# Keys of both windowed attentions made feature tile by feature tile in 4 or 6 banks, with tables and clearing on GpSimd

## The chip, the cores and the metric

One core of one Trainium2 chip runs the kernel as a single launch. The metric is the device time in microseconds (us); lower is better. The kernel before was timed in three runs.

## What is computed

Two networks of two layers each, on 512 tokens of width 1024 (all float32), one behind the other:

```python
def reference(...):
    x = first_block(x, ...)      # diff attention, swiglu, shared kv + windowed attention with sinks, swiglu
    return second_block(x, ...)  # conv mixers, conv ffn, windowed attention with context, conv ffn
```

The change lies in the two windowed attentions. The first one (`shared_kv` and `swa_sink_attention` of the first network; tag "a" in the kernel) makes keys and values of the normed 512 tokens, 4 key heads of width 64. Keys and queries are normed per head and rotated by the positions:

```python
k, v = jnp.split(rms_norm(x, kv_norm) @ w_kv, 2, axis=-1)
k = apply_rope(rms_norm(k.reshape(B, S, SW_KV_HEADS, HEAD_DIM), k_norm), cos, sin)
q = apply_rope(rms_norm((h @ w_q).reshape(...), q_norm), cos, sin)
```

The second one (`windowed_gqa`; tag "b") makes keys and values of 512 tokens and of 256 context tokens (6 token tiles of 128), without the per-head norm, and rotates only the 4 tiles of tokens:

```python
q, k, v = jnp.split(h @ w_qkv, [Q_W, Q_W + KV_W], axis=-1)
kc, vc = jnp.split(hc @ w_qkv[:, Q_W:], [KV_W], axis=-1)
```

In both, each of 16 query heads sees a window of key tiles, and a sink logit joins the softmax.

## The kernel before, in words

Five engine programs are written out by hand and meet at semaphores: SP issues the loads, PE (TensorE) multiplies, ACT (ScalarE) and DVE (VectorE) evacuate and compute, POOL (GpSimd) takes the powers for the norms. All of them walk through the list `stages` that `make_plan` (L53) writes: for the first attention a late norm, `kv` (2 weight blocks: keys, values), `q` (4 blocks), `resid`; for the second a full norm, then the same.

Every float32 product is three matmuls: the rounded (high) parts of both operands, and each high part with the other's low part. So each weight block is split before use: ACT writes `w_hi` (`split`, L658), DVE writes the rest, `w_lo` (`split`, L1193; with a gain per feature tile through `low_weights`, L1206, eight operations). `s_lo` counts the blocks whose low parts are ready, `s_mm` those whose slot can be overwritten. SP loads a block of queries once the low parts of the block before in its slot are written (L468).

`kv` on PE (L2106): 2*nt projections (nt = 4 or 6 token tiles), keys of all tiles first, then values, by `project256` (L2092): for one token tile, eight feature tiles of three matmuls with 256 columns. They alternate between banks 0 and 1, so projection n waits for the evacuation of n-2 (`kpe`). The first one waits for each feature tile of the hidden states (`s_h`). Behind projections 2 to nt PE turns the keys of a tile (`turn`, L2110: four transposes of what DVE has rotated, into banks 4 and 5), and the last turn stands at the end of the stage. The first attention's sums of squares for the norm of x (`sum_squares`, L1868) run behind projection 0; its root scales rows at the evacuation.

`kv` on ACT (L920): `split(st, 1, 1)`, then per projection a copy and a square (keys, L946 and L949) or two copies into `sw_va` and `sw_vb` (values, L953 and L955), which must have been cleared (`vzero`); the turned keys' high part (L926); the query blocks' `split` 0 ahead of the values and 1 at the end, ahead of the last turned keys.

`kv` on DVE (L1625), in this order: clearing of `sw_va` and `sw_vb` (L1629, L1630); in the first attention the rotation tables of queries and keys (`rope_tables`, L1179: 32 products of 32 columns); the negated sinks (L1640); the low parts of the value weights; then per token tile the mean squares (first attention only, L1489), the rotation (L1500, L1502, L1668), the doubled keys (L1671 or L1673) and the low part of the keys turned before (`k_low`, L1644). The low parts of query blocks 0 and 1 are made behind tile nt-2 and behind the last tile, the latter ahead of the last `k_low`.

`q` (`swa`: PE L2135, ACT L965, DVE L1693): PE waits at L2245 and L2246 for all evacuated values and all key low parts, projects query tiles 0 and 1 into bank 0, turns them, and then works in 32 half steps of scores, turned exponentials, values and the projection of a later query tile. DVE per query tile: mean squares, rotation (`rotated`, L1697), `doubled`, `q_low` (L1716), and per half step the `maxima` (L1722). Query tile 4 is the first to need query block 1.

In the full norm (DVE L1449, ACT L810), DVE forms the means, waits for the roots that GpSimd takes (L523) and PE spreads, and then makes the hidden states feature tile by feature tile (L1479, L1470).

Of the kernel before, what the change touches and what calls it, by code (L numbers as in the profile page):

```python
# [11 lines left out]
ALU = mybir.AluOpType  # L12
# [3 lines left out]
P = 128  # L16
# [5 lines left out]
HD = 64  # L22
# [30 lines left out]
def make_plan():  # L53
# [93 lines left out]
    norm(gain="final_norm", toks=SEQ, final=True)  # L147
    ring = [st for st in stages if "nb" in st]
# [18 lines left out]
def program(nc, dram, out):  # L167
    stages = make_plan()
    stack = ExitStack()
    with stack:  # L170
# [22 lines left out]
        small = sbuf("small", [P, 64])  # L193
# [17 lines left out]
        neg_sink = sbuf("neg_sink", [P, 16])  # L211
# [306 lines left out]
        def _(pool):  # L518
# [56 lines left out]

            angles()
# [3 lines left out]
            for st in stages:  # L580
# [4 lines left out]
                elif st["kind"] == "heads":  # L585
# [34 lines left out]
        def _(act):  # L620
# [189 lines left out]
            def norm(st):  # L810
                for kt in range(KT_D):
# [107 lines left out]

            def kv(st):  # L920
                S = s_swt[st["tag"]]
                nt = 6 if st["ctx"] else 4

                def turned(t):
                    act.wait_ge(S["ktr"], t + 1)
                    act.activation(sw_k[:, :, t * P:(t + 1) * P],  # L926
                                   pb[:, 4 + t % 2, :].rearrange("p (g n) -> p g n", g=4), ACT.Copy).then_inc(S["khi"], 1)
                    act.drain()
# [5 lines left out]
                split(st, 1, 1)  # L934
                if st.get("late"):
                    act.wait_ge(s_pw, st["late"]["rms0"] + 1)
                for n in range(2 * nt):
                    t = n % nt
                    if n == nt:
                        split(st["after"], 0, 0)  # L940
                        act.wait_ge(S["vzero"], 1)
                    act.wait_ge(S["kpj"], n + 1)
                    if n < nt:
                        if n >= 2:
                            act.wait_ge(S["krope"], n - 1)
                        act.activation(kv_buf(st, 512 + 256 * (n % 2), 768 + 256 * (n % 2)), pb[:, n % 2, 0:256], ACT.Copy,  # L946
                                       scale=root(t))
                        act.drain()
                        r = act.activation(kv_buf(st, 1024 + 256 * (n % 2), 1280 + 256 * (n % 2)), pb[:, n % 2, 0:256],  # L949
                                           ACT.Square, scale=root(t))  # L950
                    else:
                        at = HD * (2 * t + 1)
                        act.activation(sw_va[:, :, at:at + HD], pb[:, n % 2, 0:P].rearrange("p (g f) -> p g f", g=2), ACT.Copy,  # L953
                                       scale=root(t))
                        r = act.activation(sw_vb[:, :, at:at + HD],  # L955
                                           pb[:, n % 2, P:2 * P].rearrange("p (g f) -> p g f", g=2), ACT.Copy,
# [3 lines left out]
                    if 3 <= n <= nt + 1:  # L960
                        turned(n - 3)
# [1422 lines left out]
```

## Time and profile before

| | us |
|---|---|
| median of 3 runs | 3028.74 (3027.15 to 3029.84) |
| the profiled execution's own time | 3028.09 |
| its span in the profile | 3026.3 |
| PE busy | 2786.0 (92%) |
| DVE busy | 1836.8 (61%) |
| ACT busy | 1080.0 (36%) |
| POOL busy | 118.8 (4%) |

The mean granted clock of PE over the span is 0.955 of full speed. A busy PE in the profile is a PE with matmuls in flight. Idle time of an engine costs only where another one waits for it. The stretches of this case are the first attention's keys, values and first queries, from about 724 to 802 us of the span, and the second's, from about 2280 to 2371 us. "PEclk" is the granted clock as a share of full speed, "issue" is a wait for which the profile names no engine, and a row of the timeline gives start, duration, engine, line, operation, its tiles, and in brackets the idle time before it with the operation that ended it.

### The profile page before, as it was taken

The numbers are of one execution on the slowest core, as the hardware profiler recorded it, in microseconds if no ns is written. First come the engines' busy times: TensorE is split into PE (matmuls) and PEld (weight loads), VectorE is DVE, ScalarE is ACT, GpSimd is POOL, SyncE is SP. The second block draws the span as 40 slices with busy tenths as digits, with TensorE's granted clock in tenths as the row PEclk, the third lists the DMA queues.
The fourth block names the chain that finished last, engine by engine and source line by source line (L and its number), as shares of the span: only waits on it lengthen the run. The fifth ranks groups of instructions, "written<-read, shape, count | busy, mean of one in ns | idle before, by whom it ended". The sixth has DMA issues, their size and how long they took to land.

```text
span 3026.3 us, 41051 instructions
## 1 busy us (share of the span) xinstructions
PE 2786.0 (92%) x14220; PEld 2339.0 (77%) x14220; DVE 1836.8 (61%) x2910; ACT 1080.0 (36%) x1778; POOL 118.8 (4%) x148
## 2 busy tenths in 40 slices
PE   7999899997787999998986899999997899899998
PEld 6777788886676788887875788888886787688886
DVE  6766567676565577667996554353455455564645
ACT  5444332223565322223112232232223566352432
POOL 4111000000110000000000000000000000000000
PEclk8999999998898999998997999999998999999999
DMA  3111254452001355542110122122111000232321
GB/s 110 63 56 43 98 187 167 171 182 72 29 29 36 112 180 174 175 155 68 56 49 30 48 70 70 56 65 68 54 58 42 15 29 8 70 97 91 97 89 65
DMA packets 69314, 252.07 MB, mean 83 GB/s; under 512 B 7840, under 2 KB 10144, under 8 KB 66592
## 3 DMA queue, kind: packets, MB, share of 16 engines
q1 hardware_dynamic: 69152, 249.99, 24.5%
q8 instruction: 92, 1.51, 0.2%
q14 instruction: 70, 0.57, 0.1%
HBM read 247.87 MB, written 2.10 MB: 83 GB/s over the span
## 4 chain that ended last, share of the span: by engine, by line
PE 61%; DVE 16%; issue 15%; ACT 4%; DVEq 2%; POOLq 0%; ACTq 0%; POOL 0%; DMA 0%; SPq 0%
PE psum L1852 16%; PE psum L1851 16%; PE psum L1853 16%; DVE work L1372 4%; PE psum L2233 2%; DVE w_lo L1201 1%; ACT work L991 1%; PE psum L1991 1%; ACT sw_pt L1003 1%; PE psum L1969 1%; PE psum L1971 1%; PE psum L1970 1%; DVE neg_max L1740 1%; DVE tok_ms L1489 1%; DVE w_lo L1566 1%
## 5 line engine op out<-in xcount | busy, mean ns | idle before, releaser
L1851 PE MATMUL psum<-hx_hi,w_hi 128*128 128x512 f32 x1568 | 623.9, 398 | 28.9 <-DVE w_lo L1201 13.5
L1852 PE MATMUL psum<-hx_lo,w_hi 128*128 128x512 f32 x1568 | 625.1, 399 | 0.0
L1853 PE MATMUL psum<-hx_hi,w_lo 128*128 128x512 f32 x1568 | 623.7, 398 | 0.0
L675 ACT ACTIVATE w_hi<-w_raw 128x1024 fp32r<-128x1024 f32 (+1 forms) x328 | 344.6, 1051 | 527.2 <-PE psum L1853 231.4
L1201 DVE TENSOR_TENSOR w_lo<-w_raw,w_hi 128x1024 fp32r<-128x1024 f32 (+1 forms) x328 | 397.7, 1212 | 192.6 <-ACT w_hi L675 174.0
L1851 PEld LDWEIGHTS psum<-hx_hi,w_hi 128*128 128x128 f32 x1568 | 297.1, 189 | 79.1 <-issue 16.7
L1853 PEld LDWEIGHTS psum<-hx_hi,w_lo 128*128 128x128 f32 x1568 | 297.1, 189 | 69.9
L1852 PEld LDWEIGHTS psum<-hx_lo,w_hi 128*128 128x128 f32 x1568 | 298.0, 190 | 48.4
L1851 PE MATMUL psum<-a_hi,w_hi 128*128 128x512 f32 (+1 forms) x656 | 234.1, 357 | 18.1 <-DVE a_lo L1313 10.0
L1852 PE MATMUL psum<-a_lo,w_hi 128*128 128x512 f32 (+1 forms) x656 | 234.8, 358 | 0.0
L1853 PE MATMUL psum<-a_hi,w_lo 128*128 128x512 f32 (+1 forms) x656 | 233.9, 357 | 0.0
L1851 PE MATMUL psum<-o_hi,w_hi 128*128 128x512 f32 x544 | 217.8, 400 | 5.6 <-DVE o_lo L1778 3.9
L1852 PE MATMUL psum<-o_lo,w_hi 128*128 128x512 f32 x544 | 216.8, 398 | 0.0
L1853 PE MATMUL psum<-o_hi,w_lo 128*128 128x512 f32 x544 | 216.7, 398 | 0.0
L1335 DVE SCALAR_TENSOR_TENSOR work<-psum,vec,work 128x511 f32<-128x511 f32 (+1 forms) x132 | 83.2, 658 | 164.3 <-ACT work L758 156.3
L523 POOL TENSOR_TENSOR tok_r<-tok_ms,half 128x4 f32<-128x4 f32 (+1 forms) x70 | 71.8, 1025 | 2502.2 <-DVE tok_ms L1115 1949.6
L1277 DVE SCALAR_TENSOR_TENSOR X<-psum,mods,X 128x512 f32<-128x512 f32 x96 | 60.6, 658 | 178.6 <-PE psum L1853 177.1
L1851 PEld LDWEIGHTS psum<-a_hi,w_hi 128*128 128x128 f32 x656 | 125.2, 191 | 38.5 <-DVE a_lo L1313 10.5
L758 ACT ACTIVATE work<-psum,vec 128x768 f32<-128x768 f32 (+1 forms) x88 | 70.0, 795 | 223.5 <-PE psum L1853 215.8
L1852 PE MATMUL psum<-hc_lo,w_hi 128*128 128x256 f32 x512 | 144.8, 283 | 0.0
L1851 PE MATMUL psum<-hc_hi,w_hi 128*128 128x256 f32 x512 | 144.8, 283 | 0.0
L1853 PE MATMUL psum<-hc_hi,w_lo 128*128 128x256 f32 x512 | 144.5, 282 | 0.0
(289 smaller groups left out, 4914.2 us busy)
## 6 DMA issues: line engine op xcount, KB each, us to landing
mod_w<-in_w_mod SPq DMA_DIRECT2D x96, 512.0 KB, 3.6
w_raw<-in_fup SPq DMA_DIRECT2D x88, 512.0 KB, 4.5
w_raw<-in_cup SPq DMA_DIRECT2D x88, 512.0 KB, 3.5
w_raw<-in_fdown SPq DMA_DIRECT2D x32, 512.0 KB, 4.6
w_raw<-in_cdown SPq DMA_DIRECT2D x32, 512.0 KB, 3.5
w_raw<-in_da_qkv SPq DMA_DIRECT2D x6, 1536.0 KB, 6.5
w_raw<-in_fdown SPq DMA_DIRECT2D x16, 384.0 KB, 3.1
w_raw<-in_cdown SPq DMA_DIRECT2D x16, 384.0 KB, 3.0
```

Source lines behind the costliest of these rows:

```text
L523: pool.tensor_tensor(tok_r[:, a:b], tok_ms[:, a:b], half[:, a:b], ALU.pow).then_inc(done, 1)
L675: r = act.activation(w_hi[:, off:off + n], w_raw[:, raw:raw + n], ACT.Copy)
L758: act.activation(wk[:, s, 0:toks], ps_of(st, s, 0, toks), ACT.Copy, scale=vec[:, bass.ds(b + col, 1)]).then_inc(s_ctap, 1)
L991: r = act.activation(work[:, e:e + (w1 - w0)], psum[:, w0:w1], ACT.Exp, bias=neg_max[:, col:col + 1], scale=root, accum_out=row_sum[:, col ...
L1201: r = dve.tensor_tensor(w_lo[:, off:off + n], w_raw[:, raw:raw + n], w_hi[:, off:off + n].bitcast(F32), ALU.subtract)
L1277: r = dve.scalar_tensor_tensor(X[:, b, a:e], ps_of(st, s, a, e), mods[:, l, c, bass.ds(b + o, 1)], X[:, b, a:e], ALU.mult, ALU.add)
L1335: dve.scalar_tensor_tensor(dst[:, a + 1:e], src(a, e - 1), prev, dst[:, a + 1:e], ALU.mult, ALU.add)
L1372: dve.scalar_tensor_tensor(acc, u[:, j:j + n], w, acc, ALU.mult, ALU.add)
L1851: pe.matmul(dst, wh, xh, start=first, stop=False)
L1852: pe.matmul(dst, wh, xl, start=False, stop=False)
L1853: return pe.matmul(dst, wl, xh, start=False, stop=last)
L2233: r = pe.matmul(pb[:, 5, 0:256], v_cols(tiles[k], g, p % 2), sw_pt[:, n % 2, 256 * i:256 * i + 256], start=p % 2 == 0 and k == 0, stop=p % ...
```

## The change

Keys: PE walks over the eight feature tiles and multiplies each for all 4 or 6 token tiles, one bank per token tile, so that all key projections end together. Values: as before one token tile after the other, each into its own bank, with the turn of the key tile before behind it (now in banks 6 and 7). The last turn moves into the query stage, behind its first projection, and the wait for all values and key low parts moves behind its second. The sums of squares of the late norm run behind feature tile 3. The mark that frees the second weight slot moves from the last turn to the first query projection.

GpSimd takes over the clearing of `sw_va` and `sw_vb`, the rotation tables of the first attention's queries and keys (8 products of 128 columns instead of 32 of 32) and the negated sinks, each in an earlier stage. The low and high parts of the value weights in the second attention move ahead of the norm's wait for roots. Those of query block 0 come behind key tile 1 (ACT: ahead of tile 2), those of query block 1 into the query stage: on ACT between the first and the second turned query tile, on DVE behind the first two query tiles and ahead of the first maxima.

```diff
+    for st, after in zip(stages, stages[1:]):
+        if st["kind"] == "norm" and after["kind"] == "kv" and not st.get("late"):
+            st["kv"] = after
...
-        small = sbuf("small", [P, 64])
+        rope_g = sbuf("rope_g", [P, 2, 96])
...
-        neg_sink = sbuf("neg_sink", [P, 16])
+        neg_sink = sbuf("neg_sink", [P, 2, 16])
...
+            def rope_gains():
+                for which, (name, scale) in enumerate((("sw_q_norm", HD ** -0.5), ("k_norm", 1.0))):
+                    pool.tensor_scalar(rope_g[:, which, 0:HD], rows(name), scale, None, ALU.mult)
+                pool.drain()
+                for which in range(2):
+                    pool.tensor_scalar(rope_g[:, which, HD:96], rope_g[:, which, 32:HD], -1.0, None, ALU.mult)
+                for which, name in enumerate(("sinks1", "sinks2")):
+                    pool.tensor_scalar(neg_sink[:, which, :], rows(name), -1.0, None, ALU.mult)
+                pool.drain()
+
+            def rope_tables():
+                for which, tab in ((0, swa_tab[:]), (1, k_tab)):
...
+                    for c, h, gain in ((0, 0, g0), (0, 1, g1), (1, 0, g1_neg), (1, 1, g0)):
+                        r = pool.tensor_tensor(tab[:, c, :, h, :], gain, trig[:, c], ALU.mult)
+                r.then_inc(s_tabs, 1)
+                pool.drain()
...
+                    rope_gains()
+                    pool.memset(sw_vb[:], 0.0)
+                elif st.get("w") == "fup0_2":
+                    pool.wait_ge(s_modd, MOD_TILES)
+                    rope_tables()
+                    pool.wait_ge(s_mm, st["block0"])
+                    pool.memset(sw_va, 0.0).then_inc(s_swt["a"]["vzero"], 1)
...
+                elif st["kind"] == "kv":
+                    pool.wait_ge(s_mm, st["block0"])
+                    pool.memset(sw_va, 0.0)
+                    pool.memset(sw_vb[:], 0.0).then_inc(s_swt["b"]["vzero"], 1)
```

In the diff of ACT, `norm` begins with the split of the value weights (second attention), and `kv` and `swa` change as follows:

```diff
             def norm(st):
+                if st.get("kv"):
+                    split(st["kv"], 1, 1)
...
-                split(st, 1, 1)
                 if st.get("late"):
+                    split(st, 1, 1)
                     act.wait_ge(s_pw, st["late"]["rms0"] + 1)
                 for n in range(2 * nt):
                     t = n % nt
+                    if n == 2:
+                        split(st["after"], 0, 0)
                     if n == nt:
-                        split(st["after"], 0, 0)
                         act.wait_ge(S["vzero"], 1)
...
                     if 3 <= n <= nt + 1:
-                        turned(n - 3)
-                split(st["after"], 1, 1)
-                turned(nt - 1)
+                        keys_turned(st, n - 3)
...
                 evac_proj(0)
+                keys_turned(st["before"], (6 if st["ctx"] else 4) - 1)
+                evac_proj(1)
                 turned(0)
-                evac_proj(1)
+                split(st, 1, 1)
                 turned(1)
```

On DVE:

```diff
                 if st.get("late"):
                     return
+                if st.get("kv"):
+                    split(st["kv"], 1, 1)
                 dve.wait_ge(s_rb, st["norm0"] + 1)
...
-                dve.memset(sw_va, 0.0)
-                dve.memset(sw_vb[:], 0.0).then_inc(S["vzero"], 1)
-                if not st["ctx"]:
...
-                            rope_tables(tc, ts, gain, 1, t)
-                dve.tensor_scalar(neg_sink[:], rows("sinks2" if st["ctx"] else "sinks1"), -1.0, None, ALU.mult)
-                dve.drain()
-                split(st, 1, 1)
+                if st.get("late"):
+                    split(st, 1, 1)
+                    dve.wait_ge(s_tabs, 5)
...
-                    if t:
-                        k_low(t - 1)
-                    if t == nt - 2:
+                    if t == 1:
                         split(st["after"], 0, 0)
-                split(st["after"], 1, 1)
+                    if t >= 2:
+                        k_low(t - 2)
+                k_low(nt - 2)
                 k_low(nt - 1)
...
                     rotated(m)
                     doubled(m)
                     q_low(m)
+                split(st, 1, 1)
                 for p in range(35):
```

On PE:

```diff
-                for n in range(2 * nt):
-                    if n % nt == 0:
-                        pe.wait_ge(s_lo, st["block0"] + n // nt + 1)
-                    if n >= 2:
-                        pe.wait_ge(S["kpe"], n - 1)
...
-                    if n == 0 and st.get("late"):
+                pe.wait_ge(s_lo, st["block0"] + 1)
+                for k in range(KT_D):
+                    pe.wait_ge(s_h, 8 * (hset[0] - 1) + k + 1)
+                    w = slice(256 * k, 256 * (k + 1))
+                    for t in range(nt):
+                        if k == 0:
+                            pe.wait_ge(s_ev, st["lin0"] + 1 + (t // 2 if st["ctx"] else t))
+                        xh, xl = h_tile(k, t)
+                        dst = pb[:, t, 0:256]
+                        pe.matmul(dst, xh, w_hi[:, w], start=k == 0, stop=False)
+                        pe.matmul(dst, xl, w_hi[:, w], start=False, stop=False)
+                        r = pe.matmul(dst, xh, w_lo[:, w], start=False, stop=k == KT_D - 1)
+                        if k == KT_D - 1:
+                            r.then_inc(S["kpj"], 1)
+                    if k == 3 and st.get("late"):
                         sum_squares(st["late"])
-                    if 2 <= n <= nt:
-                        turn(n - 2)
-                turn(nt - 1)
+                pe.wait_ge(s_lo, st["block0"] + 2)
+                for t in range(nt):
+                    pe.wait_ge(S["kpe"], t + 1)
+                    project256(pb[:, t, 0:256], t, 1, s_mm if t == 0 else None).then_inc(S["kpj"], 1)
+                    if t:
+                        turn_keys(st, t - 1)
...
+                pe.wait_ge(S["kpe"], nt + 1)
+                project(0)
+                turn_keys(st["before"], nt - 1)
+                project(1)
                 pe.wait_ge(S["kpe"], 2 * nt)
                 pe.wait_ge(S["klo"], nt)
-                project(0)
-                project(1)
                 turn_q(0)
```

## Rows read from the trace of the kernel before

**Rows 1.** Windows: PE, PEld, DVE, ACT, POOL busy us (count), PEclk, DMA share, GB/s
```profile
core 0: us, PE busy (x) PEld busy (x) DVE busy (x) ACT busy (x) POOL busy (x), PEclk, DMA share, GB/s
11.40:22.40 11.00, 11.00 (x64) 10.75 (x62) 8.05 (x12) 7.46 (x14) 8.99 (x16) 1.00 0.93 358
754.30:758.90 4.60, 4.57 (x22) 4.57 (x23) 2.59 (x6) 0.95 (x2) 1.01 (x1) 0.50 0.23 98
758.90:763.20 4.30, 4.23 (x36) 4.03 (x35) 1.31 (x4) 3.01 (x7) 0.04 (x1) 1.00 0.01 4
830.30:834.40 4.10, 4.09 (x17) 3.73 (x18) 3.36 (x9) 1.91 (x5) 1.55 (x2) 0.58 0.00 0
684.00:700.00 16.00, 16.00 (x70) 12.85 (x70) 5.44 (x7) 3.94 (x6) 0.00 (x0) 1.00 0.24 75
2480.00:2500.00 20.00, 19.32 (x141) 17.23 (x140) 10.56 (x27) 12.65 (x28) 0.65 (x1) 1.00 0.01 1
724.10:799.30 75.20, 46.42 (x298) 44.67 (x298) 45.45 (x115) 23.18 (x53) 7.05 (x7) 0.75 0.17 56
2294.90:2368.40 73.50, 56.18 (x392) 53.05 (x393) 39.57 (x59) 24.70 (x48) 0.00 (x0) 0.81 0.13 44
```

**Rows 2.** Waits of PE, 724 to 800: who for whom, total us, times, longest
```profile
PE psum L2116 <- DVE kv_tmp L1671: 14.4, 2, 12.1
PE psum L2152 <- issue: 7.8, 1, 7.8
```

**Rows 3.** Waits of PE, 2280 to 2370
```profile
PE psum L2099 <- DVE hc_lo L1470: 12.7, 8, 3.8
PE psum L2152 <- issue: 5.3, 1, 5.3
```

**Rows 4.** Timeline, DVE, first attention: start us, us, operation, idle before
```profile
729.08 0.69 DVE L1274 TENSOR_TENSOR X<-psum,X 128x512 f32<-128x512 f32 x1
...
735.50 1.45 DVE L1629 MEMSET sw_va<- 128x1664 f32 x1 [0.47 <-issue]
...
747.94 3.25 DVE L1209 SCALAR_TENSOR_TENSOR w_lo<-w_raw,vec,w_hi 128x256 fp32r<-128x256 f32 x8 [0.42 <-issue]
...
751.29 0.42 DVE L1489 TENSOR_REDUCE tok_ms<-kv_tmp 128x4 f32<-128x256 f32 x1
...
754.37 0.42 DVE L1489 TENSOR_REDUCE tok_ms<-kv_tmp 128x4 f32<-128x256 f32 x1
...
801.89 0.42 DVE L1489 TENSOR_REDUCE tok_ms<-sw_sq 128x4 f32<-128x256 f32 x1
```

**Rows 5.** Timeline, ACT and DVE, first attention
```profile
736.70 0.47 ACT L949 ACTIVATE kv_tmp<-psum,tok_r 128x256 f32<-128x256 f32 x1
...
800.12 0.69 DVE L1718 TENSOR_TENSOR sw_qb<-psum,sw_qa 128x512 fp32r<-128x512 f32 x1 [1.73 <-ACT sw_qa L981]
```

**Rows 6.** Timeline, DVE and PE, second attention
```profile
2291.15 2.37 DVE L1479 SCALAR_TENSOR_TENSOR work<-X,gains,psum 128x512 f32<-128x512 f32 x4 [4.42 <-PE psum L1860]
...
2309.63 0.58 PE L2099 MATMUL psum<-w_hi,hx_hi 128*128 128x256 f32 x1 [1.46 <-DVE hc_lo L1470]
...
2310.33 0.48 DVE L1470 SCALAR_TENSOR_TENSOR hc_lo<-work,mods,hc_hi 128x256 fp32r<-128x256 f32 x1
...
2314.57 2.29 DVE L1201 TENSOR_TENSOR w_lo<-w_raw,w_hi 128x2048 fp32r<-128x2048 f32 x1
2316.95 0.42 DVE L1500 TENSOR_TENSOR work<-work,axial 128x256 f32<-128x256 f32 x1
...
2318.74 0.42 DVE L1500 TENSOR_TENSOR work<-work,axial 128x256 f32<-128x256 f32 x1
...
2370.11 0.69 DVE L1731 TENSOR_REDUCE neg_max<-psum 128x1 f32<-128x512 f32 x1
```

**Rows 7.** Lines by themselves: count, duration ns min/median/max, starts; last modulation sum
```profile
L1145 DVE TENSOR_TENSOR w_lo<-w_raw,w_hi x8: 558/810/822, 7.6 to 26.2; 128x384 fp32r<-128x384 f32 x8
...
L571 POOL TENSOR_TENSOR da_tab_c<-work,trig x4: 642/832/1432, 24.1 to 37.2; 128x128 f32<-128x128 f32 x4
...
682.75 1.22 DVE L1224 SCALAR_TENSOR_TENSOR mod_out<-mod_w,mod_c 128x1024 f32<-128x1024 f32 x1
```

More of the change, by code:

```diff
@@ L574, in head_table @@
                 pool.drain()
+            k_tab = kv_tmp[:, 2560:3072]
+            def rope_gains():
[9 more added lines that the diff above has]
+                for which, tab in ((0, swa_tab[:]), (1, k_tab)):
+                    tab = tab.rearrange("p (c t h f) -> p c t h f", c=2, t=4, h=2)
+                    g0, g1, g1_neg = (rope_g[:, which, a:a + 32].unsqueeze(1).broadcast_to([P, 4, 32]) for a in (0, 32, HD))
+                    for c, h, gain in ((0, 0, g0), (0, 1, g1), (1, 0, g1_neg), (1, 1, g0)):
+                        r = pool.tensor_tensor(tab[:, c, :, h, :], gain, trig[:, c], ALU.mult)
+                r.then_inc(s_tabs, 1)
+                pool.drain()
             angles()
@@ L918, in heads, with keys_turned @@
                 outputs_high(7)
+            def keys_turned(st, t):
+                S = s_swt[st["tag"]]
+                act.wait_ge(S["ktr"], t + 1)
+                act.activation(sw_k[:, :, t * P:(t + 1) * P],
+                               pb[:, 6 + t % 2, :].rearrange("p (g n) -> p g n", g=4), ACT.Copy).then_inc(S["khi"], 1)
+                act.drain()
             def kv(st):
@@ L1176, in modulation @@
                                                      vec[:, o:o + 8], ALU.add, ALU.mult)
-                dve.drain()
-            def rope_tables(tab_c, tab_s, gain, n, t):
-                g = gain.rearrange("p (n h f) -> p n h f", n=n, h=2)
-                cos, sin = over(trig[:, 0, t, :], n), over(trig[:, 1, t, :], n)
-                tc = tab_c.rearrange("p n (h f) -> p n h f", h=2)
-                ts = tab_s.rearrange("p n (h f) -> p n h f", h=2)
-                for h in range(2):
-                    dve.tensor_tensor(tc[:, :, h, :], g[:, :, h, :], cos, ALU.mult)
-                    dve.drain()
-                dve.scalar_tensor_tensor(ts[:, :, 0, :], g[:, :, 1, :], -1.0, sin, ALU.mult, ALU.mult)
-                dve.drain()
-                dve.tensor_tensor(ts[:, :, 1, :], g[:, :, 0, :], sin, ALU.mult)
                 dve.drain()
@@ L1695, in swa @@
                 t1, t2 = sw_t[:, 0, :], sw_t[:, 1, :]
+                sinks = neg_sink[:, 1 if st["ctx"] else 0, :]
                 def rotated(m):
@@ L2104, in project256, with turn_keys @@
                 return r
+            def turn_keys(st, t):
+                S = s_swt[st["tag"]]
+                pe.wait_ge(S["krope"], t + 1)
+                if t >= 2:
+                    pe.wait_ge(S["klo"], t - 1)
+                for g in range(4):
+                    o = 1536 + 512 * (t % 2) + P * g
+                    r = pe.transpose(pb[:, 6 + t % 2, g * P:(g + 1) * P], kv_buf(st, o, o + P), ident[:])
+                r.then_inc(S["ktr"], 1)
             def kv(st):
@@ L2108, in kv @@
                 nt = 6 if st["ctx"] else 4
-                def turn(t):
-                    pe.wait_ge(S["krope"], t + 1)
-                    if t >= 2:
-                        pe.wait_ge(S["klo"], t - 1)
-                    for g in range(4):
-                        o = 1536 + 512 * (t % 2) + P * g
-                        r = pe.transpose(pb[:, 4 + t % 2, g * P:(g + 1) * P], kv_buf(st, o, o + P), ident[:])
-                        if t == nt - 1 and g == 0:
-                            r.then_inc(s_mm, 1)
-                    r.then_inc(S["ktr"], 1)
@@ L2151, in project @@
                         dst = pb[:, 0, 0:256]
-                        pe.matmul(dst, xh, w_hi[:, off:off + 256], start=k == 0, stop=False)
+                        r = pe.matmul(dst, xh, w_hi[:, off:off + 256], start=k == 0, stop=False)
+                        if m == 0 and k == 0:
+                            r.then_inc(s_mm, 1)
                         pe.matmul(dst, xh, w_lo[:, off:off + 256], start=False, stop=False)
```

37 lines of the change are left out of this document (9 added, 28 removed).

## The prediction, made before the changed kernel ran

> **What bounds the kernel now.** The page comes first: span 3026.3 us, PE busy 92%, and a chain that is 61% PE, 16% DVE and 15% "issue". So most stretches are full and only holes in PE can be won. The two stretches that the change touches are holes: between the last block of the stage before and the first scores of the query stage PE is busy for 46.4 of 75.2 us in the first attention, at a granted clock of 0.75, and for 56.2 of 73.5 us in the second, at 0.81 [rows 1]. The waits say on whom. In the first, PE stands 14.4 us in the two transposes of turned keys behind DVE's L1671, 12.1 of it at once, and 7.8 us ahead of the first query projection [rows 2]; no engine is named there, but project(0) stands behind waits on the last key low part, and DVE gives that only behind the low parts of the second query block. In the second, 12.7 us go to the hidden states, one feature tile after the other, and 5.3 ahead of the query projection [rows 3]. The timeline says what DVE did meanwhile: from 735.50 it cleared, made tables and split weights, and took the first key tile at 751.29, though ACT had it by 737.2 [rows 4, 5].
>
> **The clock.** After each hole PE runs at 1.2 GHz first: 22 matmuls in 4.6 us (0.21 each) at clock 0.50, then 36 in 4.3 us (0.119 each) at 1.00, which is 2.4 GHz [rows 1]. I use 4.6 us at 0.21, then 0.119; another low stretch is 4.1 us [rows 1].
>
> **First attention, step by step.** PE starts the keys as before, at 726.7. Feature tile 0 now goes through four banks, and the fourth waits until the residual in bank 3 is evacuated: DVE's L1274 at 729.08 ends at 729.8 [rows 4]. Nine matmuls fit ahead; 1.9 us of idle are added here. Of the other 87, 22 run low (to 734.4), 65 take 7.7 us and the sums of squares, now after feature tile 3, 1.0: the keys end at 743.1. The first token tile is done a microsecond earlier, 742.0, some 9 us later than today. That is paid, since nothing could use it sooner. Means and roots come by 739 and DVE splits the second block (3.3 us [rows 4]) by 742.3, both ahead of it.
> ACT copies and squares a tile in 1.0 us (0.47 each and a gap [rows 5]), so DVE starts at 743.0 and not at 751.3. Its queue then sets the pace: four tiles of 3.08 us (751.29 to 754.37 [rows 4]), the first query block's low parts 3.3, and four key low parts of 0.8 each (a 512-wide difference, 0.69 [rows 5], and a gap), together 18.8: 761.8. PE's own queue meanwhile (four value projections of 24 matmuls, 2.85 each, transposes, project(0)) needs some 18 us and waits 2 to 3 us in pieces of 1, which I take as too short to lower the clock. The hole ahead of the queries is gone, as project(0) asks only for the first evacuated value.
> Then rotation of query tile 0 on DVE 2.6 (a key tile less its 0.4 us addition), transposes and ACT's copy 1.4 (DVE waited 1.73 [rows 5], and part of that was PE's other work), low part 0.8, and the same again for tile 1: 771.4. Now the moved piece: query block 1's low parts, 3.3 us, stand ahead of the first maxima, with PE behind them (scores of half 1 need the first exponentials): 774.7. Maxima 1.0: DVE rotates query tile 2 at 775.7. Today it does at 801.89 [rows 4]. **Gain 26.2.**
>
> **Second attention.** Hidden states come every 2.47 us (1.0 of matmuls and a wait of 1.46 today) and the last low part ends at 2310.8 [rows 6]; those DVE steps stay. PE did 3 matmuls for each of them, now it does 18: 22 in the first 4.6 us from 2294.9, then 122 at 0.119 = 14.5: 2314.0, which is later than the last data plus 18 matmuls (2313.0), so PE's count sets it. The low parts of block 1 (2.29 [rows 6]) move to DVE's wait for the roots (4.42 us up to 2291.15 [rows 6]) and cost nothing; without that wait they would cost 2.3. Six values and five transposes: 6 x 2.85 + 5 x 0.36 = 18.9, then project(0), one transpose and project(1) with a 0.2 us wait, 6.3: 2339.2. DVE has 15.6 us of work here (four tiles of 1.79, 2316.95 to 2318.74 [rows 6], two copies, six low parts, one 2.3 split) and is ahead. Query tiles 0 and 1 by the same chain without means (rotation 1.8, hand-over 1.4, low part 0.8; the first rotation beside project(1)): 2339.2 + 2.2 + 4.0 = 2345.4. Low parts of block 1, 2.4: first maxima at 2347.8, today 2370.11 [rows 6]. **Gain 22.3.** The stage behind is full (PE 19.3 of 20 us at clock 1.00 [rows 1]), so the shift stays.
>
> **Given back.** Ahead of the exponentials PE will stand some 3 us in both stages. After such a hole in today's first query stage it ran at clock 0.58 for 4.1 us [rows 1], worth 1.7 us of a full PE: I take 1.5 in the second and 1.0 in the first, where PE has holes anyway.
>
> **GpSimd.** No row shows a clear of this size there. DVE takes 1.45 [rows 4]; GpSimd's dearest 128x128 product takes 1.43 [rows 7], by 13 (1664 columns) 18.6. A clear lies between, and eight table products take 5 to 11 (0.64 to 1.43 each). Covers: tables and one clear start once the modulation is summed, at 684 [rows 7], and are asked for at 742; the other clear and the gains follow the heads stage, with all of a feed-forward behind them; the second attention's pair starts at 2288.2 and is asked for at 2327 (even 2 x 18.6 arrives at 2325). If that cover went, ACT and PE would wait for the difference. What they do to DVE is the unknown: the first weights' low parts took 0.56 at best and 0.81 in the median while GpSimd worked [rows 7], 45% more. Lower end 0 (a release of DVE is already counted), upper end 20 us of the second norm at 45%, 9 us. I take 0.5, since what GpSimd does there is clearing, and DVE's longest operation there reads PSUM.
> The Trainium skill, SBUF — State Buffer (Who interferes with whom), says that a VectorE instruction with two SBUF inputs contends with a GpSimd one that reads SBUF, but not with one that only writes. By that rule the term would be 0.0; the 0.56 to 0.81 beside reading GpSimd operations agrees with it, and no row shows the writing side.
>
> **Sum.** 26.2 + 22.3 - 2.5 - 0.5 = 45.5, off the profiled execution's 3028.1: 2982.6. The median of the runs is 0.6 above that execution: **2983**.
>
> **Rivals.** (a) *Keys at the low clock* (0.08). The keys now change bank after every three matmuls, and PE is fed in portions in the second attention. If it stayed at 1.2 GHz, the first keys cost 65 x 0.094 = 6.1 more and the second 144 x 0.2125 = 30.6, 11.6 more: 3000. Against it: the first projections of the kernel run the same loop, four banks, three matmuls each, and have 64 matmuls of 384 columns in 11 us at clock 1.00 [rows 1]. The Trainium skill, TensorE: Matmul & The Clock Gate (A second HAM failure mode: psum-queue depth-cycling), describes a kernel whose clock moved to and fro because PE cycled through banks; by its rule the time would be this rival's, and this trace does not bear it out.
> (b) *The new hole ahead of the first maxima lasts on* (0.07). If both query stages ran at 0.58 for 20 us and not 4, 8 us more in the full one and 4 in the other: 2995. For it: the 3.3 and 2.4 us stand ahead of everything; against: clock 1.00 a few us behind the hole in [rows 1].
> (c) *GpSimd shuts DVE out: slower* (0.03). Place: the 37 us of clears in the second norm, where DVE sets the pace, and 30 us of tables and clear at 684. There DVE is busy 5.4 of 16 us under a full PE [rows 1], which hides about 10. With every operation at its dearest and DVE stopped throughout: 37 + 20 = 57 lost against 49 won : 3036. It decides only once over 46 us are lost, five times the 9 above.
> (d) *Nothing moves* (0.02): PE is held through the evacuations or the roots so that DVE starts at 751 as before: 3029. A wait for the second block (742.3) would have to slip 9 us.
> The forecast itself has 0.80; within it the length of the low stretches (1 us either way, twice), the 1.4 us hand-over (1.7 at most, four times) and the waits in pieces give 2975 to 2990. With (b) inside and (c), (d) and most of (a) outside, the range is 2975 to 2997. A measurement of this kernel tells about 0.2%, 6 us, from no change: faster 0.95 (forecast, a, b), same 0.02, slower 0.03.
>
> **What the profile after would show.** Right: no clears or 32-wide products on DVE; the first mean of a key tile near 743; the wait behind L1671 falls from 14.4 to about 2 and that ahead of project(0) is gone; keys of the second attention in one stretch from 2295 minus the first gain to 19 us later; about 1.9 us of idle within the first feature tile; about 3 us ahead of the second scores. Wrong: clock 0.50 throughout the keys (a); 0.58 beyond 5 us in the query stages (b); clears near 18 us or DVE's norm steps longer than 2.47 a pair (c); DVE's first tile behind 746, or PE waiting for hidden states in portions as now.

## Result and profile after

| | before | changed |
|---|---|---|
| median of the runs beside each other | 3029.09 us (3027.15 to 3029.84, 4 runs) | 2992.51 us (2988.13 to 2997.06, 4 runs) |
| span of the profiled execution | 3026.3 | 2995.2 |

The ratio is 0.988 (95% interval 0.9865 to 0.9895): 36.6 us faster where 46 were forecast, inside the range. A later series of the same kernel gave 2989.73 (4 runs); the median of all eight is 2991.0.

The windows of the changed kernel, with the columns of [rows 1]: the stretch from the first key to the rotation of query tile 2 in the first attention, its slow beginning and the full stretch behind it, the stretch behind the hole ahead of the exponentials, and the second attention from its first key to its first maxima.
```profile
734.24:783.84 49.60, 41.38 (x318) 39.86 (x318) 35.11 (x77) 26.00 (x58) 7.06 (x7) 0.94 0.19 66
734.24:740.50 6.26, 5.41 (x23) 5.12 (x24) 5.53 (x8) 4.15 (x9) 0.00 (x0) 0.50 0.49 168
740.50:749.00 8.50, 8.50 (x75) 8.50 (x74) 3.42 (x9) 1.46 (x4) 1.01 (x1) 1.00 0.00 0
784.99:788.10 3.11, 2.40 (x10) 2.00 (x11) 2.09 (x7) 1.05 (x4) 0.59 (x1) 0.50 0.60 253
2285.39:2339.09 53.70, 52.07 (x414) 50.98 (x414) 35.12 (x57) 25.12 (x50) 0.00 (x0) 0.96 0.06 21
```
Both stretches took 75.21 us before (726.68 to 801.89, 2294.90 to 2370.11); they take 49.59 and 53.70 now. PE is busy for 83% of the first and 97% of the second, at a clock of 0.94 and 0.96 instead of 0.75 and 0.81 [rows 1].

Who PE waits for, 731.6 to 808 us, answering to [rows 2]:
```profile
PE psum L2192 <- DVE sw_dup L1730: 3.4, 5, 1.2
PE psum L2246 <- ACT work L1028: 3.1, 1, 3.1
PE psum L2145 <- DVE w_lo L1234: 2.5, 1, 2.5
PE psum L2129 <- DVE sw_k L1663: 1.7, 2, 0.9
```
The 14.4 and 7.8 us are gone. What is left are pieces near 1 us, the wait ahead of the first key, which was there before, and one new hole of 3.1 us ahead of the exponentials. DVE, GpSimd and PE in the timeline, answering to [rows 4, 5]:
```profile
694.02 2.43 POOL L596 TENSOR_TENSOR kv_tmp<-rope_g,trig 128x128 f32<-128x128 f32 x4
696.59 1.49 POOL L630 MEMSET sw_va<- 128x1664 f32 x1
...
734.24 0.58 PE L2145 MATMUL psum<-w_hi,hx_hi 128*128 128x256 f32 x1 [2.55 <-DVE w_lo L1234]
...
750.35 0.42 DVE L1516 TENSOR_REDUCE tok_ms<-kv_tmp 128x4 f32<-128x256 f32 x1 [2.35 <-ACT kv_tmp L988]
...
779.49 3.25 DVE L1234 SCALAR_TENSOR_TENSOR w_lo<-w_raw,vec,w_hi 128x256 fp32r<-128x256 f32 x8
782.84 0.42 DVE L1757 TENSOR_REDUCE neg_max<-psum 128x2 f32<-128x256 f32 x1
783.83 0.42 DVE L1516 TENSOR_REDUCE tok_ms<-sw_sq 128x4 f32<-128x256 f32 x1
```
DVE now waits for ACT at its first key tile instead of making tables, and the moved low parts stand directly ahead of the first maxima.

The two stages gained 25.6 and 21.5 us, 47.1 together. The span fell by 31.1 only. The table cuts each profiled span at four instructions: PE's first key of the first attention (K1), DVE's rotation of query tile 2 (Q), PE's first key of the second (K2), DVE's first maxima there (M). It holds the experiments too; the times are starts and differences of starts in us, all from the traces. The medians come from three series on three chips, and the kernel before was timed in each: 3028.3 us beside after_again, before_again, addr_shift and split_late, 3028.3 beside after_placed, aligned, pool_only and keys_only, 3030.0 beside shift64, shift512, best and undo_placed. Each ratio below is to the kernel before in its own series.

| kernel | start to K1 | K1 to Q | Q to K2 | K2 to M | M to end | median |
|---|---|---|---|---|---|---|
| before | 726.68 | 75.21 | 1493.01 | 75.21 | 656.2 | 3029.1 |
| before_again | 727.40 | 75.33 | 1493.20 | 75.12 | 656.2 | 3029.2 |
| changed | 734.24 | 49.59 | 1501.56 | 53.70 | 656.1 | 2992.5 |
| after_again | 727.20 | 50.55 | 1499.84 | 53.45 | 658.4 | 2989.7 |
| addr_shift | 731.09 | 75.94 | 1495.98 | 74.10 | 657.3 | 3035.9 |
| shift64 | 726.45 | 75.25 | 1499.00 | 75.68 | 653.9 | 3032.4 |
| shift512 | 729.80 | 75.76 | 1493.37 | 75.28 | 654.1 | 3028.1 |
| after_placed | 728.03 | 50.51 | 1493.78 | 53.47 | 656.4 | 2983.6 |
| aligned | 727.18 | 50.53 | 1496.45 | 53.54 | 653.5 | 2985.5 |
| pool_only | 731.35 | 59.81 | 1492.87 | 75.14 | 653.5 | 3012.4 |
| keys_only | 725.09 | 61.57 | 1496.55 | 53.47 | 658.5 | 2998.6 |
| split_late | 730.18 | 46.18 | 1501.43 | 51.16 | 655.2 | 2986.7 |
| best | 727.33 | 47.16 | 1496.88 | 51.08 | 656.7 | 2979.1 |
| undo_placed | 725.50 | 51.18 | 1493.73 | 54.31 | 653.6 | 2982.5 |

So the changed kernel's first profile lost 7.6 us ahead of K1 and 8.6 between Q and K2, in stages that the change does not touch. That was the first question.

### The profile page after: what moved, and what is told of

Same layout as the page of the kernel before. It is cut to its first block, busy times and chain, and to the rows that moved or that the text cites. A ratio compares the mean times of both kernels' runs of the same rounds, so it can differ in the third digit from the quotient of the medians.

```text
span 2995.2 us, 40999 instructions
## 1 busy us (share of the span) xinstructions
PE 2789.4 (93%) x14220; PEld 2338.0 (78%) x14220; DVE 1825.8 (61%) x2871; ACT 1081.1 (36%) x1778; POOL 131.6 (4%) x166
## 3 DMA queue, kind: packets, MB, share of 16 engines
q1 hardware_dynamic: 69152, 249.99, 24.7%
## 4 chain that ended last, share of the span: by engine, by line
PE 62%; DVE 16%; issue 15%; ACT 4%; DVEq 2%; POOLq 1%; POOL 0%; ACTq 0%; DMA 0%; SPq 0%
PE psum L1869 16%; PE psum L1870 16%; PE psum L1871 16%; DVE work L1397 4%; PE psum L2257 2%; DVE w_lo L1226 1%; ACT work L1028 1%; PE psum L2009 1%; ACT sw_pt L1040 1%; PE psum L1987 1%; PE psum L2246 1%; PE psum L1988 1%; PE psum L1989 1%; DVE w_lo L1593 1%; DVE tok_ms L1516 1%
```

## Experiments: where 16 us went

**The same kernels again.** No edit.

> The changed kernel once more. In its first profile the two attention stages gained 25.6 and 21.5 us, 47.1 together, but the span fell by 31.1 only: 7.6 us were gone before the keys of the first attention (between the heads stage and 734 us) and 8.6 us between the two attentions, where a block of the last feed-forward took 8.48 us instead of 8.40 at clock 1.00. Theory of chance: those 16 us belong to that one execution; a second profile shows the keys near 727 to 730 and a span near 2985. Theory of the code (placement of the buffers or of the work): both losses come again within 1 us, keys at 734 and a block of 8.48 us, and the median stays at 2990 to 2995.

Measured 2989.73 us (2986.64 to 2992.55). The theories split: the loss ahead of the keys was of that execution, the one between the attentions came again (6.8 of 8.6 us). PE's first key in the second profile of the changed kernel:
```profile
727.20 0.39 PE L2145 MATMUL psum<-w_hi,hx_hi 128*128 128x256 f32 x1 [2.55 <-DVE w_lo L1234]
```

> The kernel before once more, for the spread of its own stages. Theory of chance: its keys of the first attention start anywhere from 727 to 734 us and its block of the last feed-forward takes 8.40 to 8.48. Theory of the code: 726.7 within 1 us and 8.40 again; the time 3029 within 3 us in either case.

Measured 3029.18 us (3026.3 to 3032.82, 10 runs), ratio to its own series 1.0003 (0.9993 to 1.0012). K1 727.40 and Q to K2 1493.20: the part between the attentions repeats within 0.2 us. K1 lies between 725.1 and 734.2 in the fourteen profiles, with no order by kernel, so the first profile's 7.6 us are put down to its execution. K1 goes with the granted clock ahead of it: summed up to K1, PE stood at clock 0.50 for 54.6 us in the profiles with K1 at 725.1 and 725.5, for 58.0 in the first profile of the kernel before (726.7), and for 79.1 in the first of the changed kernel (734.2); the others lie between, in nearly this order. Why the clock differs from one execution to the next stays open.

**The kernel before with its buffers moved.** The change makes one table larger (`small`, 64 columns, becomes `rope_g`, 192) and doubles `neg_sink`; both are allocated ahead of the working tiles and the hidden states, which so move by 512 and 576 bytes. Their addresses were read from the compiled programs; the sizes of the tiles, each rounded up to 32 bytes, add up to the same place within 128 bytes.
```
-        small = sbuf("small", [P, 64])
+        small = sbuf("small", [P, 192])
-        neg_sink = sbuf("neg_sink", [P, 16])
+        neg_sink = sbuf("neg_sink", [P, 32])
```

> The kernel before with two small tables made larger, so that all later buffers lie 512 or 576 bytes further on, as they do in the changed kernel; nothing else differs. Theory that placement costs the 16 us outside the attentions: a block of the last feed-forward takes 8.48 us instead of 8.40, the keys of the first attention start near 734 us instead of 727, and the time is 3040 to 3045. Rival, that placement does nothing: 3029 within 3 us.

Measured 3035.86 us (3031.41 to 3038.86, 11 runs), ratio 1.0021 (1.0012 to 1.003): slower by 7.6 us, with the same instructions on the same shapes. That is less than the 11 to 16 expected and more than the rival's 3. The trace has only 3.0 of it between Q and K2, and 4.4 ahead of K1, which scatters by as much anyway.

**Which of the two moves.** Each line of that edit by itself.

> The kernel before with its hidden states and operands 64 bytes further on (they begin 96 bytes behind a multiple of 128, as in the changed kernel), the working tiles where they were. Theory that the place of the moving operands within 128 bytes makes the difference: a block of the last feed-forward takes 8.48 us instead of 8.40, time 3034 to 3036, like the shift of 512 and 576 bytes. Rival, that it is the 512 bytes (the working tiles, the distance to the weights): 8.40 us and 3028.

> The kernel before with working tiles and hidden states 512 bytes further on (the hidden states begin 32 bytes behind a multiple of 128, as before). Theory that the place within 128 bytes decides: 8.40 us a block and 3028. Rival, that the distance does: 8.48 us and 3034 to 3036.

Measured: 64 bytes 3032.44 us (ratio 1.0012, 1.0002 to 1.0021), 512 bytes 3028.14 us (0.9997, 0.9988 to 1.0007). The 64 bytes cost 2.5 us and not the 4 to 6 more that were expected, and 2.5 and -1.8 do not add up to the 7.6 of both together. The medians alone leave this open; the traces are sharper. DVE's weight split in a block of the feed-forward ahead of the second attention (the "last feed-forward" of the expectations), and the fiftieth split after it (one a block nearly throughout), in the kernel before, with 64 bytes, and in the changed kernel:
```profile
1738.90 1.23 DVE L1201 TENSOR_TENSOR w_lo<-w_raw,w_hi 128x1024 fp32r<-128x1024 f32 x1 [0.26 <-ACT w_hi L675]
...
2156.42 1.23 DVE L1201 TENSOR_TENSOR w_lo<-w_raw,w_hi 128x1024 fp32r<-128x1024 f32 x1 [0.18 <-ACT w_hi L675]
```
```profile
1739.50 1.23 DVE L1201 TENSOR_TENSOR w_lo<-w_raw,w_hi 128x1024 fp32r<-128x1024 f32 x1 [0.26 <-ACT w_hi L675]
...
2160.62 1.23 DVE L1201 TENSOR_TENSOR w_lo<-w_raw,w_hi 128x1024 fp32r<-128x1024 f32 x1 [0.18 <-ACT w_hi L675]
```
```profile
1723.84 1.23 DVE L1226 TENSOR_TENSOR w_lo<-w_raw,w_hi 128x1024 fp32r<-128x1024 f32 x1 [0.26 <-ACT w_hi L710]
...
2145.33 1.23 DVE L1226 TENSOR_TENSOR w_lo<-w_raw,w_hi 128x1024 fp32r<-128x1024 f32 x1 [0.18 <-ACT w_hi L710]
```
417.5, 421.1 and 421.5 us; the 8.40 and 8.48 of the expectations were read off single blocks. With 512 bytes (1742.94 to 2160.50) it is 417.6. So in this stretch the place within 128 bytes decides: the hidden states begin 32 bytes behind a multiple of 128 in the kernel before, 96 in the changed one. All fourteen profiles sort by it: 417.3 to 417.6 us in the eight at 32 bytes, 421.1 to 421.5 in the five at 96, 419.7 in the one at 0 (further down). The starts of the matmuls show where. In 407 steps of six matmuls each (512, 512, 512, 256, 256, 256 columns), with PE at clock 1.00 and no waits, a step takes 1.050 us on average in every profile at 32 bytes and 1.060 in every one at 96; the first of the six has most of it (0.230 against 0.237). Over the stretch's some 400 steps that is the 4 us.

From that last split to K2 the profiles sort the same way: 138.3 to 138.7 us at 32 bytes, 140.0 to 140.1 at 96. The first part of Q to K2, up to the first of the splits, takes 934.5 to 941.0 us with no order by place. So the column Q to K2 mixes two things: the place, worth 5.2 us between after_again and after_placed (3.6 and 1.6), and a scatter of several us that is not explained. keys_only and best have the old place and still show 1496.6 and 1496.9.

**The changed kernel with every buffer where it was.** The two tables go behind the last buffer.
```
-        rope_g = sbuf("rope_g", [P, 2, 96])
+        small = sbuf("small", [P, 64])
-        neg_sink = sbuf("neg_sink", [P, 2, 16])
+        neg_sink1 = sbuf("neg_sink", [P, 16])
...
+        _, rope_g, neg_sink2 = layout(("tail_gap", [P, 24 * D], F32), ("rope_g", [P, 2, 96], F32), ("neg_sink2", [P, 16], F32))
```

> The changed kernel with its two new tables put behind the last buffer, so that every other buffer lies at the address that it has in the kernel before; the instructions are the same. The kernel before with its buffers shifted took 7.6 us more, and its feed-forward of both token sets took 8.48 us a block where the kernel before took 8.40, as in the changed kernel. Theory that this placement took back 6 us of the gain: a block takes 8.40 us again, the time is 2984 to 2985 against the 2991 of the changed kernel (median of its 8 runs so far). Rival, that the loss comes with the changed program itself (code, queues): 8.48 us and 2990.

Measured 2983.6 us (2983.01 to 2984.12), ratio 0.9852 (0.9837 to 0.9867). 50 splits take 417.5 again and Q to K2 1493.8: the theory of placement holds.
```profile
1716.38 1.22 DVE L1228 TENSOR_TENSOR w_lo<-w_raw,w_hi 128x1024 fp32r<-128x1024 f32 x1 [0.26 <-ACT w_hi L712]
...
2133.87 1.23 DVE L1228 TENSOR_TENSOR w_lo<-w_raw,w_hi 128x1024 fp32r<-128x1024 f32 x1 [0.19 <-ACT w_hi L712]
```

**Would a full boundary be better still?**
```
         sw_sum = sbuf("sw_sum", [P, 4])
+        pad = sbuf("pad", [P, 8])
```

> The changed kernel with one unused tile of 32 bytes more ahead of the hidden states, which so begin at a multiple of 128 bytes; before they begin 32 bytes behind one, in the changed kernel 96. Theory that a matmul's reading costs more where its data begin off such a boundary: the six matmuls of a step of the feed-forward of both token sets, 1.057 us before and 1.065 changed, take 1.05 or less, the pure 512-column stages gain too, and the time is below 2985. Rival, that only the order of addresses against the weights matters and 32 bytes do nothing: 1.065 us and 2991.

Measured 2985.46 us (2983.01 to 2993.21), no gain over the 2983.6 at 32 bytes. 50 splits take 419.7 us and a step of six matmuls 1.055, both between the other two places, so there theory and rival missed. But where all matmuls have 512 columns the theory was right in most stages. The same splits in the feed-forward behind the second attention, first in after_placed (70.62 us), then here (70.34):
```profile
2745.04 1.23 DVE L1228 TENSOR_TENSOR w_lo<-w_raw,w_hi 128x1024 fp32r<-128x1024 f32 x1 [0.16 <-issue]
...
2815.66 1.23 DVE L1228 TENSOR_TENSOR w_lo<-w_raw,w_hi 128x1024 fp32r<-128x1024 f32 x1 [0.51 <-ACT w_hi L712]
```
```profile
2744.99 1.22 DVE L1227 TENSOR_TENSOR w_lo<-w_raw,w_hi 128x1024 fp32r<-128x1024 f32 x1 [0.17 <-issue]
...
2815.33 1.23 DVE L1227 TENSOR_TENSOR w_lo<-w_raw,w_hi 128x1024 fp32r<-128x1024 f32 x1 [0.51 <-ACT w_hi L711]
```
Six matmuls of 512 columns without a wait take 1.400 us at clock 1.00 in all thirteen profiles at 32 or 96 bytes. At 0 they take 1.394 from 950 to 1390 us and from 2650 to 2990, but 1.400 from 350 to 730, where the hidden states lie at the same place. So the fastest place for the mixed stage is not the one for the even stages, and the place alone does not set the pace. By an estimate from these numbers the even stages win some 3 us at 0 and the mixed one loses as much. Why is open: 32 and 96 stand the same to a multiple of 64 and still differ in the mixed stage, so a line of 64 bytes read once more is not it.

## Experiments: what each part of the change is worth

**GpSimd's part alone** (buffers in place): the kernel before without the clears and tables at the head of DVE's key stage, and with the changed kernel's GpSimd code.
```
-                dve.memset(sw_va, 0.0)
-                dve.memset(sw_vb[:], 0.0).then_inc(S["vzero"], 1)
...
+                dve.wait_ge(s_tabs, 5)
```

> The kernel before with the tables, clears and sinks on GpSimd as in the change, its two new tables behind the last buffer; the keys are made token tile by token tile and the low parts stay where they were. Theory: DVE reaches the first key tile of the first attention some 12 us sooner (739.3 instead of 751.3), the wait of PE behind L1671 falls from 14.4 to 2 or 3 us and no other wait takes its place, gain 11 to 12; nothing in the second attention; 3017. Rival, that PE's own sequence holds it next: 5 us or less, 3023.

Measured 3012.43 us (3011.57 to 3017.64), ratio 0.9951 (0.9937 to 0.9965): a gain of 15.9. K1 to Q falls by 15.4, K2 to M by nothing. The waits of PE, 720 to 806 us:
```profile
PE psum L2175 <- issue: 7.8, 1, 7.8
...
PE psum L2139 <- DVE kv_tmp L1693: 2.3, 1, 2.3
```
14.4 fell to 2.3 as expected: 12.1. The other 3 us go with the clock. Over the stage (K1 to Q) it is 0.83 and not 0.75, and PE is busy for 44.6 us with the same 307 matmuls that took 47.8 before (47.0 in before_again). The theory had left that term out. The stage before and in this kernel:
```profile
726.68:801.89 75.21, 47.83 (x307) 45.96 (x308) 44.36 (x112) 25.38 (x57) 7.05 (x7) 0.75 0.17 56
731.35:791.15 59.80, 44.57 (x307) 42.95 (x308) 35.08 (x76) 25.39 (x57) 7.05 (x7) 0.83 0.21 71
```

**The order alone** (tables, clears and sinks back on DVE, at the head of its key stage; buffers in place).
```
+                dve.memset(sw_va, 0.0)
+                dve.memset(sw_vb[:], 0.0).then_inc(S["vzero"], 1)
...
-                dve.wait_ge(s_tabs, 5)
```

> The changed kernel with tables, clears and sinks back on DVE at the head of the key stage, and every buffer where it is before: so only the order of keys, turns and low parts is changed. Theory: in the first attention DVE takes the first key tile 24 us after PE's first key, as before (16 in the changed kernel), what follows it is as short as in the changed kernel (33.5 us instead of 50.6 to the rotation of query tile 2), gain 17; in the second 21.5; sum 38.5 and 2990. Rival, that with DVE late the rest is not short either: the first attention gains under 10, 2997 or more.

Measured 2998.57 us (2997.04 to 3003.83), ratio 0.9907 (0.9892 to 0.9923): 29.8 us gained, where 38.5 and 2990 were expected. The second attention gave 21.7, all that the whole change gives there; the first 13.6, not 17. DVE takes the first key tile at 752.71, 27.6 us after K1 and so 3 later than expected (the means wait for four feature tiles of keys: 11.2 us after K1, before 8.2), and the low parts of the value weights stand behind the tables too, so that the value projections wait for them:
```profile
749.36 3.26 DVE L1216 SCALAR_TENSOR_TENSOR w_lo<-w_raw,vec,w_hi 128x256 fp32r<-128x256 f32 x8 [0.42 <-issue]
...
752.67 0.58 PE L2109 MATMUL psum<-w_hi,hx_hi 128*128 128x256 f32 x1 [10.64 <-DVE w_lo L1216]
```
```profile
742.00:752.60 10.60, 0.03 (x1) 0.00 (x0) 8.25 (x35) 1.03 (x3) 0.00 (x0) 0.74 0.00 2
752.60:758.00 5.40, 5.33 (x27) 5.33 (x28) 4.50 (x12) 4.25 (x10) 2.01 (x2) 0.55 0.59 197
```
Behind that hole PE runs at 0.55 for 5.4 us. By the medians the parts add up to 15.9 + 29.8 = 45.7 against 44.7 for both at the same addresses (3028.3 to 2983.6), but by the stages they do not: in the first attention 15.4 and 13.6 stand against 24.7 for both together, so 4.3 us can be had by either part. The medians agree only because keys_only loses elsewhere what its stages gain: they gave 35.3 us, and its profile is 3.6 us longer from Q to the first of the 50 splits and 2.4 longer behind M. Why is open; it is not the place, since its 50 splits take 417.5.

**The low parts of the second query block, two half tiles later than the change puts them.** They are needed by project(4) at the third half tile only.
```
                     q_low(m)
-                split(st, 1, 1)
...
                         sink_args(m)
+                    if p == 1:
+                        split(st, 1, 1)
```

> DVE's low parts of the second query block are made two half tiles later, ahead of the low parts of query tile 2, where DVE waits 1.95 us in the first attention and 3.33 in the second for ACT. Theory that the 3.25 and 2.29 us stand on the path to the first maxima: the first stage gains 3.25 less the 1.3 that do not fit into the wait, the second 2.3, the hole of PE ahead of the first exponentials stays near 3 but comes earlier, sum 4.2 us: 2988 against 2992.5. Rival, that PE is held there by its own projections and transposes: no gain, 2992.

Measured 2986.69 us (2985.66 to 2988.48) against 2989.73 of the same kernel without the edit in the same series; 2991.0 with the earlier runs. That is 3.0 to 4.3 against the 4.2 expected, but it is little against runs that spread by 6, so it was run once more at the good addresses.

> Both findings together: the changed kernel with its two tables behind the last buffer, and DVE's low parts of the second query block two half tiles later. If the two add up, 2983.6 less the 4.3 us that the later low parts took off the changed kernel (2991.0 to 2986.7): 2979, and 6 less by the profile's stages (3.0 in the first attention, 3.3 in the second): 2977 to 2980. If the later low parts gained only because of where the buffers lay: 2983.

Measured 2979.08 us (2977.51 to 2980.87, 5 runs), ratio 0.9834 (0.982 to 0.9847), against 2983.6 (highest 2980.87 below lowest 2983.01, though the kernel before was 1.6 us slower beside this run): the two add up. DVE and PE in the first attention of this kernel:
```profile
778.48 3.26 DVE L1236 SCALAR_TENSOR_TENSOR w_lo<-w_raw,vec,w_hi 128x256 fp32r<-128x256 f32 x8
781.83 0.69 DVE L1737 TENSOR_TENSOR sw_qb<-psum,sw_qa 128x512 fp32r<-128x512 f32 x1
```
```profile
PE psum L2177 <- DVE w_lo L1236: 1.1, 1, 1.1
...
PE psum L2249 <- ACT work L1030: 0.8, 1, 0.8
```
project(4) waits 1.1 us for the low parts, and the wait ahead of the exponentials is 0.8 (1.8 in after_placed, 3.1 in the changed kernel's first profile). K1 to Q flatters this kernel, as Q now stands ahead of the low parts. Fairer is how far the same ACT instructions lie ahead of the kernel before: from 1740 to 2400 us, that is across the second attention, the lead grows from 22.6 to 42.3 us in after_placed and from 23.4 to 47.7 here. So most of the 4.5 us comes from the second attention, where DVE had waited 3.33 us at that place in the changed kernel's first profile.

**And put back to where they were before the change.**
```
# ACT and DVE, end of the key stage
+                split(st["after"], 1, 1)
# ACT and DVE, query stage
-                split(st, 1, 1)
```

> The changed kernel with its two tables behind the last buffer and the low parts of the second query block put back to the end of the key stage on ACT and DVE, as before the change. Theory: the change's third part (low parts later) cost time where it was put, ahead of the first maxima. Put back, they wait for the first query projection in the first attention (ACT 3.3, then DVE 3.25) and delay the query turns by about 2 us, but the 3.25 ahead of the maxima go: gain 1.3; in the second attention they fit into DVE's free time beside the first two projections: gain 2.3; sum 3.6 and 2980. Rival, that the later place was right, since DVE is the queue that sets the pace either way: 2983.6 or more.

Measured 2982.5 us (2980.13 to 2984.44), ratio 0.9847 (0.9834 to 0.9861), against 2983.6: 1.1 us less, within what runs on two chips tell apart, so the medians alone would not rule out the 3.6. The traces speak against it: K1 to Q is 0.7 longer and K2 to M 0.8. The hole ahead of the exponentials goes, as expected, but PE pays for it earlier, in the waits of 765 to 800 us of this kernel and ahead of project(1) (2.22 us, behind ACT's 3.30 of high parts):
```profile
PE psum L2194 <- DVE sw_dup L1733: 3.7, 5, 1.5
PE psum L2176 <- ACT sw_sq L1015: 2.2, 3, 1.2
...
PE psum L2248 <- ACT work L1031: 0.3, 1, 0.3
```
So as it was made this part of the change gave nothing that these runs show. Two half tiles on it is worth 4.5 us, and 3.4 against this kernel, which ran beside best (2982.5 and 2979.08).

## Why the prediction was right, and where it was not

- **The sum within the stages** was 26.2 + 22.3; measured 25.6 and 21.5 (24.7 and 21.7 at the old addresses). The keys took 15.9 us from PE's first key, forecast 16.4. The wait for bank 3 was 0.85 us in this profile and not 1.9, as the nine matmuls ahead of it ran at clock 0.50 and lasted to 736.5. In after_again and after_placed they ran at full clock as forecast; there the wait was 1.7 and the keys took 16.9. DVE was held to ACT's first tile, then its own queue of 3.08 a tile set the pace, as forecast. The hand-overs took 1.38 to 1.44, taken as 1.4. The second attention's keys ran on without a wait for 19.4 us, forecast 19.1; two windows from them:
```profile
2286.00:2292.00 6.00, 6.00 (x37) 6.00 (x37) 5.54 (x11) 2.75 (x5) 0.00 (x0) 0.65 0.01 3
2292.00:2306.00 14.00, 14.00 (x121) 14.00 (x120) 10.50 (x20) 6.49 (x13) 0.00 (x0) 1.00 0.00 1
```
- **Given back** by the clock behind the new hole: taken as 1.0 and 1.5. The lead over the kernel before, taken at the same ACT instructions, shrinks behind the holes by 0.8 and 0.9 us in the first profile, by 0 and 1.0 in after_again, by 0 and 2.0 in after_placed. The low stretch is there (clock 0.50 from 784.99, window above) and short; rival (b) falls.
- **GpSimd** was bounded from 1.45 to 18.6 us a clear. It took 1.49, and the table products 0.6 each: both at the lower end, and the second pair was over at 2281.5, before DVE's first step of the second norm at 2281.67. Those steps stayed at 2.47 us a pair. Rival (c) falls, and with it the 0.5 us. One DVE instruction with two SBUF inputs did stand beside a clear for its last 1.1 us, the low parts at 2277.34, and took 2.33 us against 2.29 [rows 6]. The Trainium skill, SBUF — State Buffer (Who interferes with whom), lets a write-only GpSimd instruction run beside such a one without contention; those 0.04 us agree with it.
- **Rival (a)**, keys at the low clock, falls: 121 matmuls in 14.0 us at clock 1.00, three to a bank, in the rows above. The Trainium skill, TensorE: Matmul & The Clock Gate (A second HAM failure mode: psum-queue depth-cycling), would have had the clock move to and fro; no run here shows it.
- **Rival (d)** falls with the first key tile 16.1 us after K1 instead of 24.6.
- **The step that failed** is none of these but one that was not in the sum: "the stage behind is full ..., so the shift stays", with all that lies between the attentions costed at nothing. Two enlarged tiles in the change's own diff moved the hidden states by 576 bytes. That slowed the stages ahead of K2 by 5.2 us (after_again against after_placed, 3.6 in the 50 splits and 1.6 behind them), and the medians differ by 7.4 (2991.0 and 2983.6); the other 2.2 are not located. The rest of the distance between 2983 and 2992.5 is scatter, as in the late K1 of the first profile.
- **In part it was luck** that the kernel at the old addresses takes 2983.6 where 2983 was forecast. The stages gave 46.4 us and not 48.5, and what was taken off was near 2.0 and not 3.0, so two misses cancel by half. At the new addresses the result lies in the range because the range reached 14 us up, for reasons (rival (b)) that did not come true.

## What to carry over

Cost a change's allocations as well as its instructions: a tile that grows moves every buffer behind it, and a full matmul stage can feel that by 1% (421.5 against 417.5 us). Put new small tiles behind the large operands, and compare a stage that the change does not touch between the two traces, part by part and in more than one profile of each, before looking for a cause in the one that it does. In this kernel a hole of 12.1 us in PE cost its length and some 3 us more at low clock behind it, so closing it paid more than the wait that the profile shows. Two parts of a change that shorten the same stage can each claim the same microseconds; add them up by stage, not by median. And work taken from the head of a queue should go to a place where that queue waits: the same 3 us of low parts cost about as much ahead of the first maxima as they had at the end of the key stage, and little ahead of a wait of 2 to 3 us.

## What the hardware showed

- The start address of the moving operands within 128 bytes changes the pace of matmuls at clock 1.00. In the stage that alternates three matmuls of 512 and three of 256 columns, six take 1.050 us at 32 bytes (eight profiles), 1.055 at 0 (one) and 1.060 at 96 (five). Where all have 512 columns, six take 1.400 at 32 and 96, and at 0 1.394 in two of the three long stages and 1.400 in the other. The cause is open.
- A clear of 128x1664 f32 takes GpSimd 1.49 us, as long as DVE's 1.45 [rows 4].
- The same instructions reach K1 at 734.2 us in one execution of the changed kernel and at 727.2 in another, after 79.1 and 58.0 us at clock 0.50.
- A hole of 12.1 us costs more than itself: without it the same 307 matmuls kept PE busy for 44.6 us instead of 47.8, at a mean clock of 0.83 instead of 0.75.
